# A fused encoder layer on one core: half of the attention's probability tiles turned by VectorE blocks and a trip through DRAM

## Chip, cores and metric

The kernel is one program on one core of a Trainium2 chip. The metric is the time of one execution on the device, in microseconds (us).

## What is computed

One hybrid encoder layer on 1024 tokens of width 1024, in float32. The change is in the second of its token mixers, attention over 8 heads:

```python
k_b = jnp.concatenate([k_nope, k_rope], axis=-1)
q_b = rmsnorm(q_b, q_head_norm)
k_b = rmsnorm(k_b, k_head_norm)
...
def attend(qblk):
    s = jnp.einsum('bhqd,bhkd->bhqk', qblk, k_t).astype(jnp.float32) * scale
    p = jax.nn.softmax(s, axis=-1)
    return jnp.einsum('bhqk,bhkd->bhqd', p.astype(v_t.dtype), v_t)
```

Around it stand, in this order: the latent projections, this attention, a gated linear attention (GLA) of 4 heads, the merge of both branches, and a mixture of 16 experts, which takes the largest share of the time.

## The kernel before

The kernel is written engine by engine: each engine has its own program, and engines wait for each other's counters (semaphores). Nothing is scheduled by a tool, so the order on each queue is the order of the code. SP's queue only issues DMAs, and a wait in it holds up every DMA behind it. P is 128, HALF 512, NT 8 tiles of 128 tokens, MH 8 heads.

Matmuls take each operand as a high and a low part (fp32r), three products for one: `three` (L1108 to L1110). So every operand has a `_hi` tile, rounded by ScalarE (ACT), and a `_lo` tile, the difference, made by VectorE (DVE) in `low_part` (L1719).

The attention loop goes over STEPS: (i, n) is head i, query tile n; tile t = 8i + n; five more steps (8, 0) to (8, 4) drain it. In one step:

- PE (TensorE) makes the scores of tile t, 10 matmuls of 128x512 into two PSUM banks (`scores`); transposes one piece of the coming head's q or k (`seam`); transposes the eight 128x128 blocks of tile t - 2 (`probs_T`, L1097); runs some key tiles of the product with the values of a finished half head (`values`, 3 matmuls a key tile); and projects a piece of a later head (`project`). In the drain, `project_qk` starts the GLA stage.
- DVE takes the row maximum of tile t (`row_maximum`, L1954), makes low parts, and in `normalise` (L1960, L1961) divides tile t - 1 by its row sums.
- ACT copies the transposed tile to pT_hi (`probs_high`, L2797) and makes the exponentials with the row sums (`exponentials`, L2805). A tile of probabilities is in one of three buffers.
- `head_out` copies a finished half head to obS, and SP stores it (`store_ob`, L794).

In the last head, SP loads the layer's input rows again, as one DMA of 4 MB (L810, `hT_again`, shown as carry), and the first GLA weights (d_raw, L742). At steps (7, 6) and (8, 0) ACT makes `dense_hi` and `rows_high` of them, DVE `dense_lo` and `rows_low`. After the last store of attention output, GpSimd (POOL) builds constants for GLA, for which PE waits.

The functions that the diff touches:

## Time and profile before

| | us |
|---|---|
| median of 3 runs | 1935.23 |
| lowest, highest | 1934.19, 1937.03 |
| the profiled execution's own time | 1936.58 |
| its span in the profile | 1934.7 |

The profile shows one execution. Its span is the time from the first to the last instruction; the time outside it is 1.9 us. The attention loop lies between some 123 and 538 us. Busy times of PE are modelled from a pipeline in which matmuls overlap, so the distance between starts tells the cost of one, not its length. The rows below are from a breakdown by stretch, from the list of waits, from groups of like instructions, and from the timeline.

### The profile page before, as it was taken

The page shows a single profiled execution, that of the slowest core. Times are in us where ns is not written, and L with a number is a line of the kernel's source. Part 1 is how long each engine was busy: PE and PEld are TensorE (multiplying, and loading weights), DVE is VectorE, ACT ScalarE, POOL GpSimd, SP SyncE. Part 2 cuts the span into 40 slices and gives each one's busy share as a digit, 9 for nine tenths or more (in the row PEclk, how much of TensorE's full clock was granted, in tenths as well). Part 3 has the DMA queues.
Part 4 walks back from the last instruction along what each step waited for, and adds up shares of the span by engine and source line. Part 5 has one row for each costly group of instructions (what it writes and reads, how often), then busy time and mean ns, then how long its engine had stood idle before and what let it go on. Part 6 is the DMA issues. An engine that isn't in the chain of part 4 may idle for free.

```text
span 1934.7 us, 27125 instructions
## 1 busy us (share of the span) xinstructions
PE 1885.0 (97%) x9427; PEld 1598.3 (83%) x9427; DVE 1388.8 (72%) x1941; ACT 1066.4 (55%) x1768; POOL 135.8 (7%) x147
## 2 busy tenths in 40 slices
PE   8999999999999999999999999995999999999998
PEld 8988888888878888888888888884788888888886
DVE  4578777777855656556866348746799898998986
ACT  6576565655552434344534123324677777877775
POOL 1021111011000000000000000000000101001010
PEclk9999999999999999999999999997999999999999
DMA  6110000000321202021353553534999999999993
GB/s 209 44 43 7 23 18 23 23 18 26 121 66 33 64 25 66 22 77 65 120 176 131 178 192 109 175 142 181 359 400 400 391 401 393 396 400 390 399 391 77
DMA packets 147482, 327.58 MB, mean 169 GB/s; under 512 B 18080, under 2 KB 72736, under 8 KB 147232
## 3 DMA queue, kind: packets, MB, share of 16 engines
q1 hardware_dynamic: 141600, 309.59, 43.0%
q0 software_dynamic: 4752, 16.78, 3.4%
q8 instruction: 57, 0.93, 0.2%
q14 instruction: 33, 0.27, 0.0%
q10 hardware_dynamic: 1040, 0.00, 0.0%
HBM read 287.92 MB, written 38.40 MB: 169 GB/s over the span
## 4 chain that ended last, share of the span: by engine, by line
PE 91%; DVE 5%; ACT 2%; issue 1%; DMA 1%; POOL 1%; SPq 0%; DVEq 0%; ACTq 0%; POOLq 0%
PE ps L1108 24%; PE ps L1110 24%; PE ps L1109 24%; PE ps L1097 7%; PE ps L1195 3%; PE ps L1403 1%; PE ps L1234 1%; PE ps L1233 1%; PE ps L1415 1%; PE ps L1387 1%; PE ps L1413 1%; DVE affT L2571 1%; DMA xs<-in_x 1%; DVE top_v L2564 0%; DVE pT_lo L1719 0%
## 5 line engine op out<-in xcount | busy, mean ns | idle before, releaser
L1719 DVE TENSOR_TENSOR w_lo<-w_raw,w_hi 128x1024 fp32r<-128x1024 f32 x384 | 442.7, 1219 | 54.8 <-ACT w_hi L3173 54.6
L3173 ACT ACTIVATE w_hi<-w_raw 128x1024 fp32r<-128x1024 f32 x384 | 371.1, 1053 | 0.4 <-PE ps L1110 0.4
L1108 PE MATMUL ps<-w_hi,xeT_hi 128*128 128x512 f32 x512 | 201.2, 393 | 1.0 <-DVE w_lo L1719 0.9
L1110 PE MATMUL ps<-w_hi,xeT_lo 128*128 128x512 f32 x512 | 199.7, 390 | 0.0
L1109 PE MATMUL ps<-w_lo,xeT_hi 128*128 128x512 f32 x512 | 199.2, 389 | 0.0
L1719 DVE TENSOR_TENSOR d_lo<-d_raw,d_hi 128x1024 fp32r<-128x1024 f32 (+1 forms) x66 | 67.1, 1027 | 124.5 <-ACT d_hi L2814 119.9
L1108 PE MATMUL ps<-hT_parts,d_hi 128*128 128x512 f32 x368 | 145.3, 395 | 0.0
L1110 PE MATMUL ps<-hT_parts,d_lo 128*128 128x512 f32 x368 | 143.9, 391 | 0.0
L1109 PE MATMUL ps<-hT_parts,d_hi 128*128 128x512 f32 x368 | 143.8, 391 | 0.0
L1015 POOL TENSOR_TENSOR stat<-stat,minus_half 128x4 f32<-128x4 f32 (+3 forms) x56 | 54.3, 971 | 1176.5 <-DVE stat L1716 1176.4
L1954 DVE TENSOR_REDUCE row_max<-ps 128x1 f32<-128x1024 f32 x64 | 78.3, 1224 | 79.1 <-PE ps L1234 79.0
L2814 ACT ACTIVATE d_hi<-d_raw 128x1024 fp32r<-128x1024 f32 x42 | 44.6, 1062 | 136.3 <-PE ps L1110 79.2
L1108 PEld LDWEIGHTS ps<-w_hi,xeT_hi 128*128 128x128 f32 x512 | 96.1, 188 | 21.3 <-DVE w_lo L1719 1.2
L1110 PEld LDWEIGHTS ps<-w_hi,xeT_lo 128*128 128x128 f32 x512 | 96.1, 188 | 20.4
L1108 PE MATMUL ps<-d_hi,hT_parts 128*128 128x512 f32 x288 | 112.6, 391 | 0.0
L1109 PEld LDWEIGHTS ps<-w_lo,xeT_hi 128*128 128x128 f32 x512 | 96.2, 188 | 19.5
L1109 PE MATMUL ps<-d_lo,hT_parts 128*128 128x512 f32 x288 | 112.1, 389 | 0.0
L1110 PE MATMUL ps<-d_hi,hT_parts 128*128 128x512 f32 x288 | 112.1, 389 | 0.0
L1108 PE MATMUL ps<-w_hi,act_T_hi 128*128 128x512 f32 x256 | 101.3, 396 | 0.8 <-ACT ye L3196 0.8
L1110 PE MATMUL ps<-w_hi,act_T_lo 128*128 128x512 f32 x256 | 99.9, 390 | 0.0
L1109 PE MATMUL ps<-w_lo,act_T_hi 128*128 128x512 f32 x256 | 99.6, 389 | 0.0
L1719 DVE TENSOR_TENSOR pT_lo<-ps,pT_hi 128x512 fp32r<-128x512 f32 x128 | 82.0, 682 | 0.7 <-ACT pT_hi L2797 0.2
(451 smaller groups left out, 4363.3 us busy)
## 6 DMA issues: line engine op xcount, KB each, us to landing
w_raw<-in_w_gate_e SPq DMA_DIRECT2D x128, 512.0 KB, 7.4
w_raw<-in_w_up_e SPq DMA_DIRECT2D x128, 512.0 KB, 7.1
w_raw<-in_w_down_e SPq DMA_DIRECT2D x128, 512.0 KB, 6.6
d_raw<-in_w_in SPq DMA_DIRECT2D x80, 256.0 KB, 3.3
gates_T<-stage SPq DMA_DIRECT2D x16, 512.0 KB, 2.7
sg<-gates_T SPq DMA_DIRECT2D x16, 512.0 KB, 3.7
stage<-mla_out_T SPq DMA_DIRECT2D x12, 512.0 KB, 5.2
xs<-in_x SPq DMA_DIRECT2D x8, 512.0 KB, 12.8
```

Source lines behind the costliest of these rows:

```text
L1015: pool.tensor_tensor(dst, dst, minus_half[:, 0:dst.shape[1]], ALU.pow).then_inc(done, 1)
L1097: ins = pe.transpose(ps[0:rows, bank, j * P:(j + 1) * P], src, ident[:])
L1108: pe.matmul(out_ap, a_hi, b_hi, start=start, stop=False)
L1109: pe.matmul(out_ap, a_hi, b_lo, start=False, stop=False)
L1110: return pe.matmul(out_ap, a_lo, b_hi, start=False, stop=stop)
L1195: mm = pe.matmul(out_ap, src[:, k, toks], w[:, k, :], start=k == 0, stop=k == kc - 1)
L1233: pe.matmul(bank, qr_T[:, q], kr_T[i % 2][:, cols], start=False, stop=False)
L1234: mm = pe.matmul(bank, qr_T[:, q], kr_lo[i % 2][:, cols], start=False, stop=True)
L1719: return dve.tensor_tensor(dst, whole, high.bitcast(F32), ALU.subtract)
L1954: dve.tensor_reduce(row_max[:, n:n + 1], ps[:, 2 * (n % 2):2 * (n % 2) + 2, :], mybir.AxisListType.XY, ALU.max, negate=True).then_inc(max_ ...
L2814: nc.scalar.activation(d_hi[:, n % 2, :], d_raw[:, n % 2, :], ACT.Copy).then_inc(d_hi_ok, 1)
L3173: nc.scalar.activation(w_hi[:, n % RING, :], w_raw[:, n % RAW, :], ACT.Copy).then_inc(hi_ok, 1)
```

## The change

Tiles with an even number up to 60 (31 of 64, `by_dma`) are no longer transposed by PE. DVE transposes their 32x32 blocks within each group of 32 partitions (`probs_squares`) into squares_T; SP stores squares_T to DRAM with four DMAs, one for each group of 32 partitions, and, when they have landed, loads the tile back from there in its turned order straight into pT_lo (`turn_probs`). Two steps later ACT rounds it to pT_hi (`turned_high`) and DVE makes pT_lo in place (`turned_low`). The other 33 tiles go on through PE, one step earlier than before (tile t - 1 at step t). pT_hi and pT_lo get a new layout, 16 groups of 32 queries outside, key tiles inside, so that `values` reads its 512 columns as 16 runs of 32.

`normalise` is gone. The inverses of the row sums are made for four tiles at once (`inverse_sums`), stored to DRAM, spread from there over all partitions (`store_inverse`, `spread_inverse`), and `head_out` multiplies with them. There are two buffers of probabilities in place of three. The rows for GLA are loaded as eight DMAs, each issued when the one before has landed (`load_rows`), and the first d_raw loads are issued at step (7, 6). Some counters of later stages reuse counters of the loop, which changes no order.

The core of the diff; left out are the declarations of semaphores, the reused counters, and waits that only take the new counts:

```diff
-def tile_at(i, n):
-    return 8 * i + n - 2 if 0 <= 8 * i + n - 2 < 8 * MH else None
+def by_dma(t):
+    return 0 <= t < 8 * MH - 2 and t % 2 == 0
+def by_tensor(t):
+    return 0 <= t < 8 * MH and not by_dma(t)
...
-                        probs = sb_in(head_mem, "probs", [P, 3, S])
-                        pT_hi = sb_in(head_mem, "pT_hi", [P, 2, NT, HALF], F32R)
-                        pT_lo = sb_in(head_mem, "pT_lo", [P, 2, NT, HALF], F32R)
+                        probs = sb_in(head_mem, "probs", [P, 2, S])
+                        squares_T = sb_in(head_mem, "squares_T", [P, Q4, NT, SQ])
+                        pT_hi = sb_in(head_mem, "pT_hi", [P, 2, Q4 * Q4, NT, SQ], F32R)
+                        pT_lo = sb_in(head_mem, "pT_lo", [P, 2, Q4 * Q4, NT, SQ], F32R)
...
+        def probs_part(tile, t):
+            q = t % NT
+            return tile[:, q // Q4, Q4 * (q % Q4):Q4 * (q % Q4) + Q4]
+        def inverse_at(h, half):
+            if (h, half) == (MH - 1, 1):
+                return squares_T[:, 0:2].rearrange("p j c a -> p (j c a)")
+            return obS[:]
...
+            def turn_probs(t):
+                d, group = t // 2, t // Q4
+                sp.wait_ge(sq_ok, d + 1)
+                rows = p_dram[d % SLOTS].rearrange("(j b) q x -> b j q x", b=SQ)
+                for q in range(Q4):
+                    sp.dma_start(rows[:, :, q, :],
+                                 squares_T[q * SQ:(q + 1) * SQ].rearrange("b j c a -> b j (c a)")).then_inc(p_out, 16)
+                sp.wait_ge(p_out, 16 * Q4 * (d + 1))
+                if d:
+                    sp.wait_ge(p_in, 16 * d)
+                if group >= 2:
+                    sp.wait_ge(pv_mm, group - 1)
+                sp.dma_start(probs_part(pT_lo, t).bitcast(F32),
+                             p_dram[d % SLOTS].rearrange("p q (c a) -> p q c a", a=SQ)).then_inc(p_in, 16)
+            def store_inverse(h, half):
+                m = 2 * h + half
+                sp.wait_ge(inv_ok, m + 1)
+                if m:
+                    sp.wait_ge(inv_in, 16 * m)
+                sp.dma_start(inv_dram[half].rearrange("(t p) -> p t", p=P), row_inv[:, Q4 * half:Q4 * half + Q4],
+                             allow_slow_non_contiguous=True).then_inc(inv_out, 16)
+            def spread_inverse(h, half):
+                m = 2 * h + half
+                sp.wait_ge(inv_out, 16 * m + 16)
+                if m and m < 2 * MH - 1:
+                    sp.wait_ge(ob_out, 16 * m)
+                sp.dma_start(inverse_at(h, half), spread(inv_dram[half], HALF)).then_inc(inv_in, 16)
+            def load_rows(k):
+                if k == 0:
+                    sp.wait_ge(h_out, 32)
+                    sp.wait_ge(seam_tr, MH * 8)
+                else:
+                    sp.wait_ge(hT_in, 16 * k)
+                sp.dma_start(hT_again[:, k, :], h_dram[k]).then_inc(hT_in, 16)
+            load_ukv(2)
+            for i, n in STEPS:
+                if i < MH and by_dma(8 * i + n - 1):
+                    turn_probs(8 * i + n - 1)
+                if (i, n) == (MH - 2, 0):
                     sp.wait_ge(prj_mm, group_count(MH - 1, 7))
                     sp.wait_ge(gate_io.sem, gate_io.at(16))
                     sp.dma_start(gateT[0:STACK].bitcast(F32), gate_dram).then_inc(gate_io.sem, 16)
-                if i:
+                if n == 0 and i:
+                    store_inverse(i - 1, 1)
+                    if i == MH:
+                        spread_inverse(i - 1, 1)
+                if n == 2 and i:
                     store_ob(i - 1, 0)
-                if i + 2 < MH:
-                    load_uq(i + 2)
-                if i == MH - 1:
-                    sp.wait_ge(h_out, 32)
-                    sp.wait_ge(seam_tr, MH * 8)
-                    sp.dma_start(hT_again, h_dram.rearrange("k p s -> p k s")).then_inc(hT_in, 16)
-                if i:
-                    store_ob(i - 1, 1)
-            load_gla(0, 0)
-            load_gla(0, 1)
-            store_ob(MH - 1, 0)
+                    if i < MH:
+                        spread_inverse(i - 1, 1)
+                if n == 4:
+                    if i + 2 < MH:
+                        load_uq(i + 2)
+                    if i + 3 < MH:
+                        load_ukv(i + 3)
+                    if i < MH:
+                        store_inverse(i, 0)
+                    if 0 < i < MH:
+                        store_ob(i - 1, 1)
+                if n == 6:
+                    spread_inverse(i, 0)
+                if n == 6 and i == MH - 1:
+                    load_gla(0, 0)
+                    load_gla(0, 1)
+                if n % 2 == 0 and 8 * (MH - 1) + 2 <= 8 * i + n:
+                    for k in range(2):
+                        if 8 * i + n - 8 * (MH - 1) - 2 + k < KD:
+                            load_rows(8 * i + n - 8 * (MH - 1) - 2 + k)
             store_ob(MH - 1, 1)
...
             def probs_T(t):
-                pe.wait_ge(p_ok, t + 1)
+                pe.wait_ge(exp_ok, t + 1)
+                before = [u for u in range(t) if by_tensor(u)]
                 for b in range(2):
-                    if t:
-                        pe.wait_ge(pt_lo, 2 * t + b - 1)
+                    if before:
+                        pe.wait_ge(pt_lo, parts_count(before[-1]) - 1 + b)
                     else:
                         pe.wait_ge(seam_lo, seam_count(0, 1) + b)
-                    transpose4(4 + b, P, [probs[:, t % 3, (4 * b + j) * P:(4 * b + j + 1) * P]
+                    transpose4(4 + b, P, [probs[:, t % 2, (4 * b + j) * P:(4 * b + j + 1) * P]
                                           for j in range(4)]).then_inc(p_tr, 1)
...
-                               pT_hi[:, half, k, :], pT_lo[:, half, k, :], k == 0, k == NT - 1)
+                               pT_hi[:, half, :, k, :], pT_lo[:, half, :, k, :], k == 0, k == NT - 1)
...
-                if tile_at(i, n) is not None:
-                    probs_T(tile_at(i, n))
+                if by_tensor(8 * i + n - 1):
+                    probs_T(8 * i + n - 1)
...
-            def normalise(t):
-                n = t % NT
+            def inverse_sums(h, half):
+                m = 2 * h + half
+                dve.wait_ge(exp_ok, NT * h + Q4 * half + Q4)
+                if m >= 2:
+                    dve.wait_ge(inv_out, 16 * (m - 1))
+                at = slice(Q4 * half, Q4 * half + Q4)
+                dve.reciprocal(row_inv[:, at], row_sum[:, at]).then_inc(inv_ok, 1)
+            def probs_squares(t):
                 dve.wait_ge(exp_ok, t + 1)
-                s.link(dve.reciprocal(row_inv[:, n:n + 1], row_sum[:, n:n + 1]))
-                dve.tensor_scalar(probs[:, t % 3, :], probs[:, t % 3, :], row_inv[:, n:n + 1], None,
-                                  ALU.mult).then_inc(p_ok, 1)
+                if t:
+                    dve.wait_ge(p_out, 16 * Q4 * (t // 2))
+                dve.transpose(squares_T[:], probs[:, t % 2, :].rearrange("p (c j b) -> p j c b", c=NT, j=Q4)) \
+                    .then_inc(sq_ok, 1)
             def probs_low(t):
                 q = t % NT
                 for b in range(2):
-                    dve.wait_ge(pt_hi, 2 * t + b + 1)
-                    at = (slice(None), q // 4, slice(4 * b, 4 * b + 4), slice((q % 4) * P, (q % 4 + 1) * P))
-                    low_part(pT_lo[at], ps[:, 4 + b, :].rearrange("p (a c) -> p a c", a=4),
-                             pT_hi[at]).then_inc(pt_lo, 1)
+                    dve.wait_ge(pt_hi, parts_count(t) - 1 + b)
+                    part = probs_part(pT_lo, t)[:, :, 4 * b:4 * b + 4].rearrange("p q k a -> p k q a")
+                    high = probs_part(pT_hi, t)[:, :, 4 * b:4 * b + 4].rearrange("p q k a -> p k q a")
+                    low_part(part, ps[:, 4 + b, :].rearrange("p (k q a) -> p k q a", k=4, q=Q4), high).then_inc(pt_lo, 1)
+            def turned_low(t):
+                dve.wait_ge(pt_hi, parts_count(t))
+                low = probs_part(pT_lo, t)
+                low_part(low, low.bitcast(F32), probs_part(pT_hi, t)).then_inc(pt_lo, 1)
             def head_out(h, j):
                 dve.wait_ge(pv_mm, 2 * h + j + 1)
                 if h or j:
                     dve.wait_ge(ob_out, 32 * h + 16 * j)
-                dve.tensor_copy(obS[:], ps[:, 6, :]).then_inc(ob_ev, 1)
+                dve.wait_ge(inv_in, 32 * h + 16 * j + 16)
+                dve.tensor_tensor(obS[:], ps[:, 6, :], inverse_at(h, j), ALU.mult).then_inc(ob_ev, 1)
...
-            END_STEP = (MH - 1, 7)
             for i, n in STEPS:
-                if (i, n) == END_STEP:
-                    probs_low(tile_at(i, n))
+                t = 8 * i + n
+                if by_dma(t - 1):
+                    probs_squares(t - 1)
                 if i < MH:
                     row_maximum(i, n)
                     if seam_at(i, n):
                         seam_low(*seam_at(i, n))
-                if tile_at(i, n) is not None and (i, n) != END_STEP:
-                    probs_low(tile_at(i, n))
-                if tile_at(i, n + 1) is not None and (i, n) not in (END_STEP, (MH, 0)):
-                    normalise(tile_at(i, n + 1))
-                if (i, n) in ((MH - 1, 6), END_STEP):
-                    normalise(tile_at(i, n + 2))
+                if by_tensor(t - 1):
+                    probs_low(t - 1)
+                if by_dma(t - 3):
+                    turned_low(t - 3)
+                if n == 0 and i:
+                    inverse_sums(i - 1, 1)
+                if n == 4 and i < MH:
+                    inverse_sums(i, 0)
...
             def probs_high(t):
-                q = t % NT
                 for b in range(2):
-                    act.wait_ge(p_tr, 2 * t + b + 1)
-                    at = (slice(None), q // 4, slice(4 * b, 4 * b + 4), slice((q % 4) * P, (q % 4 + 1) * P))
-                    nc.scalar.activation(pT_hi[at], ps[:, 4 + b, :].rearrange("p (a c) -> p a c", a=4),
+                    act.wait_ge(p_tr, 2 * tensor_count(t) - 1 + b)
+                    part = probs_part(pT_hi, t)[:, :, 4 * b:4 * b + 4].rearrange("p q k a -> p k q a")
+                    nc.scalar.activation(part, ps[:, 4 + b, :].rearrange("p (k q a) -> p k q a", k=4, q=Q4),
                                          ACT.Copy).then_inc(pt_hi, 1)
+            def turned_high(t):
+                act.wait_ge(p_in, 16 * (t // 2) + 16)
+                nc.scalar.activation(probs_part(pT_hi, t), probs_part(pT_lo, t).bitcast(F32), ACT.Copy).then_inc(pt_hi, 1)
             def exponentials(i, n):
                 t = 8 * i + n
                 act.wait_ge(max_ok, t + 1)
-                if t >= 3:
-                    act.wait_ge(p_tr, 2 * (t - 3) + 2)
-                nc.scalar.activation(probs[:, t % 3, :].rearrange("p (a c) -> p a c", a=2),
+                if by_dma(t - 2):
+                    act.wait_ge(sq_ok, (t - 2) // 2 + 1)
+                elif t >= 2:
+                    act.wait_ge(p_tr, 2 * tensor_count(t - 2))
+                if i and n % Q4 == 0:
+                    act.wait_ge(inv_ok, 2 * i - 1 + n // Q4)
+                nc.scalar.activation(probs[:, t % 2, :].rearrange("p (a c) -> p a c", a=2),
...
-                if tile_at(i, n) is not None:
-                    probs_high(tile_at(i, n))
+                t = 8 * i + n
+                if by_tensor(t - 1):
+                    probs_high(t - 1)
+                if by_dma(t - 3):
+                    turned_high(t - 3)
```

Three places in the queues, at the end of the loop. First DVE, in head 7. pT_lo, d_lo and hT_parts are low parts. Before, from the row maximum of tile 62:

```order
L1954 TENSOR_REDUCE row_max<-ps 128x1 [waits s_mm]
L1719 TENSOR_TENSOR pT_lo<-ps,pT_hi 128x4x128 [waits pt_hi] x2
L1960 RECIPROCAL row_inv<-row_sum 128x1 [waits exp_ok]
L1961 TENSOR_SCALAR probs<-probs,row_inv 128x1024 [waits head_step]
L1960 RECIPROCAL row_inv<-row_sum 128x1 [waits exp_ok]
L1961 TENSOR_SCALAR probs<-probs,row_inv 128x1024 [waits head_step]
L1719 TENSOR_TENSOR d_lo<-d_raw,d_hi 128x1024 [waits d_hi_ok]
L1988 SCALAR_TENSOR_TENSOR hT_parts<-carry,g_mix_c,hT_parts 128x1024 [waits hT_hi_ok]
L1719 TENSOR_TENSOR pT_lo<-ps,pT_hi 128x4x128 [waits pt_hi] x2
L1954 TENSOR_REDUCE row_max<-ps 128x1 [waits s_mm]
L1960 RECIPROCAL row_inv<-row_sum 128x1 [waits exp_ok]
```

With the change, from the block transpose of tile 60:

```order
L2057 STREAM_TRANSPOSE squares_T<-probs 128x1024 [waits p_out,exp_ok]
L2042 TENSOR_REDUCE row_max<-ps 128x1 [waits s_mm]
L1807 TENSOR_TENSOR pT_lo<-pT_lo,pT_hi 128x1024 [waits pt_hi]
L2042 TENSOR_REDUCE row_max<-ps 128x1 [waits s_mm]
L1807 TENSOR_TENSOR pT_lo<-ps,pT_hi 128x4x4x32 [waits pt_hi] x2
L1807 TENSOR_TENSOR d_lo<-d_raw,d_hi 128x1024 [waits d_hi_ok]
L2090 SCALAR_TENSOR_TENSOR hT_parts<-carry,g_mix_c,hT_parts 128x1024 [waits hT_hi_ok]
L2042 TENSOR_REDUCE row_max<-ps 128x1 [waits s_mm]
L1807 TENSOR_TENSOR pT_lo<-ps,pT_hi 128x4x4x32 [waits pt_hi] x2
L1807 TENSOR_TENSOR pT_lo<-pT_lo,pT_hi 128x1024 [waits pt_hi]
L1807 TENSOR_TENSOR pT_lo<-ps,pT_hi 128x4x4x32 [waits pt_hi] x2
L2051 RECIPROCAL row_inv<-row_sum 128x4 [waits inv_out,exp_ok]
```

The scalings of probs are gone, the row maximum of tile 63 stands behind d_lo and hT_parts as before, and the low parts of tile 61 have moved ahead of d_lo, those of tile 62 behind that row maximum.

Second, SP's queue. carry is the rows' buffer (hT_again), obS the attention output. Before, from the stores of heads 5 and 6 on:

```order
L794 DMA mla_out_T<-obS 128x512 x3
L810 DMA carry<-rows_T 128x8x1024
L794 DMA mla_out_T<-obS 128x512
L742 DMA d_raw<-in_w_in 128x4x128 x4
L794 DMA mla_out_T<-obS 128x512 x2
L742 DMA d_raw<-in_w_in 128x2x256 x8
L770 DMA w_a<-in_gla_wa_f 16x128 x3
```

With the change, from the store of head 6's second half on:

```order
L829 DMA mla_out_T<-obS 128x512
L867 DMA carry<-rows_T 128x1024 x2
L836 DMA probs_T<-squares_T 32x4x256 x4
L843 DMA pT_lo<-probs_T 128x1024
L859 DMA obS<-inverse_sums 128x512
L777 DMA d_raw<-in_w_in 128x4x128 x4
L867 DMA carry<-rows_T 128x1024 x2
L851 DMA inverse_sums<-row_inv 128x4x1
L859 DMA squares_T<-inverse_sums 128x512
L867 DMA carry<-rows_T 128x1024 x2
L829 DMA mla_out_T<-obS 128x512 x2
L777 DMA d_raw<-in_w_in 128x2x256 x8
```

The first d_raw loads, which stood right behind the store of head 6's second half, now stand behind two loads of rows, the whole turn of tile 60 and a spread of inverse sums, and the last two stores of obS stand behind the last rows.

Third PE, the last transposes of probs. Before, from the middle of the first project_qk:

```order
L1108 MATMUL ps<-hT_parts,d_hi 128x512 [waits exp_ok]
L1109 MATMUL ps<-hT_parts,d_hi 128x512
L1110 MATMUL ps<-hT_parts,d_lo 128x512
L1108 MATMUL ps<-hT_parts,d_hi 128x512
L1109 MATMUL ps<-hT_parts,d_hi 128x512
L1110 MATMUL ps<-hT_parts,d_lo 128x512
L1097 MATMUL ps<-ident,probs 128x128 [waits pt_lo,p_ok]
L1097 MATMUL ps<-ident,probs 128x128 x3
L1097 MATMUL ps<-ident,probs 128x128 [waits pt_lo]
L1097 MATMUL ps<-ident,probs 128x128 x3
L1108 MATMUL ps<-pT_hi,v_hi 128x512
```

With the change, from the last key tile of step (7, 7):

```order
L1195 MATMUL ps<-pT_hi,v_hi 128x512
L1196 MATMUL ps<-pT_lo,v_hi 128x512
L1197 MATMUL ps<-pT_hi,v_lo 128x512
L1184 MATMUL ps<-ident,probs 128x128 [waits pt_lo,exp_ok]
L1184 MATMUL ps<-ident,probs 128x128 x3
L1184 MATMUL ps<-ident,probs 128x128 [waits pt_lo]
L1184 MATMUL ps<-ident,probs 128x128 x3
L1195 MATMUL ps<-pT_hi,v_hi 128x512
```

The transposes of tile 63 stood behind project_qk; they now stand ahead of it and directly behind the values of step (7, 7), and wait for the exponential in place of the scaled tile.

## Rows read from the trace of the kernel before

**Rows 1.** The page: busy time of each engine, and the chain that ended last, by engine.
```profile
PE 1885.0 (97%) x9427; PEld 1598.3 (83%) x9427; DVE 1388.8 (72%) x1941; ACT 1066.4 (55%) x1768; POOL 135.8 (7%) x147
...
PE 91%; DVE 5%; ACT 2%; issue 1%; DMA 1%; POOL 1%; SPq 0%; DVEq 0%; ACTq 0%; POOLq 0%
```

**Rows 2.** Busy time by stretch (us, instructions), then granted clock, DMA share, GB/s.
```profile
165.00:480.00 315.00, 314.53 (x1865) 278.90 (x1864) 242.05 (x441) 186.86 (x479) 33.30 (x24) 1.00 0.07 21
480.00:495.00 15.00, 15.00 (x86) 12.77 (x85) 14.11 (x27) 8.10 (x15) 0.00 (x0) 1.00 0.00 1
511.00:546.00 35.00, 32.47 (x160) 26.24 (x159) 26.62 (x34) 20.41 (x28) 3.62 (x6) 0.99 0.28 83
```

**Rows 3.** The waits, 127 to 527 us: in total, times, longest.
```profile
DVE row_max L1954 <- PE ps L1234: 79.0, 54, 3.6
...
PE ps L1097 <- DVE probs L1961: 0.7, 2, 0.5
```

**Rows 4.** Groups by line and form, 127 to 527 us: busy us, mean ns, idle before.
```profile
L1719 DVE TENSOR_TENSOR pT_lo<-ps,pT_hi 128x512 fp32r<-128x512 f32 x126 | 80.7, 682 | 0.7 <-ACT pT_hi L2797 0.2
L1954 DVE TENSOR_REDUCE row_max<-ps 128x1 f32<-128x1024 f32 x64 | 78.3, 1224 | 79.1 <-PE ps L1234 79.0
...
L2797 ACT ACTIVATE pT_hi<-ps 128x512 fp32r<-128x512 f32 x126 | 68.1, 597 | 13.1 <-PE ps L1097 13.0
L1097 PE MATMUL ps<-ident,probs 128*128 128x128 f32 x504 | 65.7, 273 | 1.1 <-DVE probs L1961 0.7 <-DVE pT_lo L1719 0.4
...
L1961 DVE TENSOR_SCALAR probs<-probs,row_inv 128x1024 f32<-128x1024 f32 x64 | 49.1, 767 | 2.3
...
L1960 DVE RECIPROCAL row_inv<-row_sum 128x1 f32<-128x1 f32 x64 | 9.8, 154 | 1.3 <-ACT probs L2805 1.3
...
L1910 DVE TENSOR_TENSOR qR<-qR,q_cos 128x128 f32<-128x128 f32 x14 | 4.0, 288 | 0.2
```

**Rows 5.** The chain that ended last, end of the loop: start, us, what.
```profile
506.57 0.88 PE ps L1097 x8
...
537.76 0.70 DVE obS L1976
```

**Rows 6.** Timeline of PE in step 58: start us, us, engine, line, operation.
```profile
495.91 1.03 PE L1097 MATMUL ps<-ident,probs 128*128 128x128 f32 x8
496.70 0.48 PE L1108 MATMUL ps<-pT_hi,v_hi_even 128*128 128x512 f32 x1
497.02 0.39 PE L1109 MATMUL ps<-pT_lo,v_hi_even 128*128 128x512 f32 x1
```

**Rows 7.** Timeline of DVE, end of the loop.
```profile
518.71 1.22 DVE L1719 TENSOR_TENSOR d_lo<-d_raw,d_hi 128x1024 fp32r<-128x1024 f32 x1
```

**Rows 8.** Timeline of ACT, end of the loop.
```profile
517.22 1.07 ACT L2814 ACTIVATE d_hi<-d_raw 128x1024 fp32r<-128x1024 f32 x1
```

**Rows 9.** Timeline of SP's queue, end of the loop.
```profile
495.86 0.32 SPq L794 DMA_DIRECT2D mla_out_T<-obS  x1
...
510.88 2.13 SPq L742 DMA_DIRECT2D d_raw<-in_w_in  x4
```

**Rows 10.** DMA issues of the whole span: count, KB each, median us to landing.
```profile
d_raw<-in_w_in SPq DMA_DIRECT2D x80, 256.0 KB, 3.3
...
mla_out_T<-obS SPq DMA_DIRECT2D x16, 256.0 KB, 2.2
...
carry<-rows_T SPq DMA_DIRECT2D x4, 512.0 KB, 5.3
...
pos_i<-in_positions SPq DMA_DIRECT2D x1, 4.0 KB, 4.3
```

**Rows 11.** Busy time by stretch, around two waits of PE.
```profile
543.00:545.10 2.10, 0.17 (x2) 0.04 (x1) 1.26 (x2) 1.06 (x1) 1.41 (x2) 1.00 0.30 104
545.10:548.98 3.88, 3.88 (x10) 3.05 (x11) 2.42 (x2) 1.54 (x2) 0.00 (x0) 0.56 0.00 0
...
134.90:137.00 2.10, 0.45 (x2) 0.01 (x1) 1.93 (x2) 2.05 (x11) 0.00 (x0) 1.00 0.64 221
```

72 lines of the change are left out of this document (42 added, 30 removed).

## Prediction

> **What bounds the kernel now.** I read the page's busy shares first: TensorE (PE) is busy 97% of the span and is 91% of the chain that ended last [rows 1]. The attention loop is the stretch that the change edits, so I then read the busy time by stretch [rows 2]: from 165 to 480 us PE is busy 314.5 of 315 us, VectorE (DVE) 242, ScalarE (ACT) 187, and the DMA share is 0.07. So whatever leaves PE's queue there is gained, as long as nothing else grows into the wait. The waits say the same from the other side: row_max waited 79.0 us for PE's scores in 54 of 64 tiles, while PE waited 0.7 us for the normalised tiles [rows 3]. The reader should look at two places where the cover is thin: 480 to 495 us, where PE's steps are short and DVE is busy 14.1 of 15 us, and the end of the loop, 511 to 546 us, where PE is idle 2.5 us in all [rows 2].
>
> **What is removed from PE.** The transposes of a tile are eight matmuls. Their mean of 273 ns overlaps the next ones [rows 4]; the price is the piece in the chain, 0.88 us for eight [rows 5], and the same comes from start times: transposes start at 495.91, the next matmul at 496.70 and the one after at 497.02, where the usual distance is 0.23, so 0.79 + 0.32 - 0.23 = 0.88 [rows 6]. I take 0.87. Tiles 0, 2, ..., 60 go by DMA: 31 tiles, 31 x 0.87 = 27.0 us.
>
> **What changes on DVE and ACT.** For a pair of tiles DVE loses two scalings (0.77 each) and two reciprocals (0.15) [rows 4], 1.8 us. It swaps one pair of 0.68 pT_lo pieces for one 1024-wide subtraction: 1.22 by the d_lo row of the same form [rows 7], so -0.1. It gains one 32x32-block transpose of 128x1024, which no row shows. Its bounds are 0.77 (one source, 1024 wide) and 2.5 (twice the 1.22 of a 1024-wide reduction, if four-byte elements went at half rate); I take 1.25, since reduction and subtraction, 1024 elements each, both cost 1.22. Sum: -0.7 us a pair. ACT swaps two 0.60 copies for one of about 1.06 (the d_hi row [rows 8]): nothing. So with 0.87 off PE and 0.7 off DVE, both shrink together over most of the loop and the 79 us of slack stay. The permuted writes of pT_hi and pT_lo have runs of 32 elements. The q_cos rows have such runs (4 of 32) and cost 0.29 us for 128 elements; contiguous 1024 cost 1.22, which makes 1.04 ns an element and 0.16 fixed, and the 512-wide pT_lo rows of 0.68 lie on the same line [rows 4, 7]. Short runs add nothing that shows: nothing.
>
> The Trainium skill ("VectorE: DVE Perf Modes", The three transpose paths) gives 311 ns for a 128x128 bf16 block transpose on VectorE and 390 ns on TensorE, and advises TensorE for a full 128x128. By eight of its figures the new instruction would be an estimated 2.5 us and DVE would gain 0.6 us a pair in place of losing 0.7; by its figure for TensorE the removed work would look like 3.1 us, which this trace refutes with 0.88 for the pipelined eight [rows 5].
>
> **The round trip through DRAM.** Per tile SP issues four stores and a load. One issue is about 0.35 us (0.32 for the store of mla_out_T [rows 9], which has as many pieces), and that 256 KB store lands in 2.2 us [rows 10]. Trip: 4 x 0.35 + 2.2 + 0.35 + a 512 KB load; 256 KB loads of d_raw land in 3.3 us [rows 10], I take 3.5: 7.5 us. The tile is turned at the head of step t+1 and wanted on ACT in step t+3. A step is now some 5.7 us (315 us for about 51 tiles is 6.2, less half of 0.87). From the end of the scores of t: exponential done at about 3.7, block transpose at 5.2, and the copy on ACT is due at 3 x 5.7 + 0.6 = 17.7. That leaves 12.5 us for 7.5. In the short steps after 480 us (10 us a pair now, 9.1 after) it is still 3 x 4.6 + 0.6 - 5.2 = 9.2. The single buffer squares_T and the in-order SP queue hold too: what stands ahead of each turn waits only for work of the step before. Hidden, at nothing. The sums' store has 512 four-byte pieces; the nearest row is pos_i, 1024 of them, 4.3 us to landing [rows 10]. It has three steps of cover; at the end it is issued at about 528 and its spread has landed by 537, three before the last output copy wants it. Nothing.
>
> **480 to 495 us.** A pair of steps is 10 us on PE and 9.4 on DVE. After: 9.1 and 8.7, with DVE's queue in order and its transpose ahead of row_max. Average cover is 0.4 us a pair. I charge 1.0 us here and for the DVE-bound first five steps together (0 if the cover holds, 3 if the transpose costs 2.5).
>
> **The end of the loop.** Here I follow the new order, on the clock of the kernel before. At 493.6 (495.91 less ten matmuls of 0.23 [rows 6]) step 58 begins; 28 turned tiles lie behind, a lead of 28 x 0.87 = 24.4 us. With 2.3 us for scores, 0.7 for each key tile of values and 0.87 for transposes: the scores of 60 end at 505.6, of 61 at 510.1, of 62 at 512.4. DVE: row_max(60) to 506.8, exponential to 508.8, block transpose(60) to 510.0, row_max(61) to 511.3, exponential to 512.6. PE waits 0.2, transposes 61, does two key tiles (514.9), scores 63 (517.2), transposes 62 and two key tiles: 519.5. Then its next work is the transposes of 63; before, it had values and project_qk in between.
> What is late is exp(63). The first d_raw load, which was issued at 510.88 [rows 9], now stands on SP behind tile 60's turn: stores from 510.0 to 511.4, landed 513.6, load and spread issued 514.3, two d_raw issues of 0.53 (2.13/4 [rows 9]) 515.4, landed with 3.5 us at 518.9. ACT makes d_hi (520.0) and hT_hi (521.1), DVE d_lo (521.2) and hT_lo (522.4), and only then comes row_max(63), to 523.6, and exp(63), to 524.9. PE is idle 5.4 us. From there: transposes 0.87, two key tiles 1.4, project_qk 2.8, two key tiles 1.4, project_qk 2.8, eight key tiles 5.6: 539.8, where before they ended at 537.6 (the output copy starts at 537.76 [rows 5]). The end costs 2.2 of the lead of 24.4. The tail behind it (output copy, store, POOL's constants) moves as a whole.
> An idle PE also costs clock: with 0.17 us of work in 543.0 to 545.1 the granted clock in the next 3.88 us was 0.56, the lower level of 1.2 GHz, and eight matmuls took about 0.43 in place of 0.23 each, 1.6 us; with 0.45 of work in 134.9 to 137.0 it stayed at 1.00 [rows 11]. 5.4 us is the longer gap by far, so I charge 1.6.
>
> **Sum.** 24.4 - 2.2 - 1.0 - 1.6 = 19.6 us. The profiled execution took 1936.6 for a span of 1934.7, so it would read 1917.0 with a span of 1915.1. The median of the runs shown is 1935.2, 1.4 below it; the forecast on that scale is 1915.6, say 1916. Stages behind shift unchanged: what they load is released by their own progress.
>
> **Rivals.**
> - *The gap at the end is shorter* (0.12). If d_raw lands early, exp(63) still stands behind the two copies and two subtractions: about 2 us idle and no fall of the clock. For it speaks that landings of 3 us are usual; against it SP's order. Gain 19.6 + 3.4 + 1.6 = 24.6: 1910 or 1911.
> - *DVE becomes the bound in short steps* (0.08). A block transpose of 2.5 us costs 0.6 us a pair over today; over most of the loop PE's 11.5 us a pair still covers DVE's 10, but in the last head's steps and the first ones, and in the gap at the end, 3 to 5 us are lost more: 1920.
> - *The round trip is late* (0.07). If stores and loads landed in 5.3 us, as 512 KB loads of rows_T did later in the program [rows 10], the trip is 1.75 + 10.6 = 12.4 us: level with the normal steps' 12.5 and 3.2 us late in some five short ones, 16 us: 1932. Every further microsecond costs some 25 us. Against it: the DMA share of 0.07.
> - *PE reads the turned layout more slowly* (0.09), the one on the other side. The values matmuls now read 16 runs of 32 columns that lie 1 KB apart. 384 matmuls are touched, 0.233 us apart now; at 0.051 us more each the gain is gone, at twice the time they add 384 x 0.233 = 89 us and the kernel takes 2005. No matmul of this trace reads such an operand, so nothing bounds it but that.
> The Trainium skill ("Advanced Engine Details and Errata", SBUF Cachelines) puts a penalty on accesses that find a new 16-byte line each time and says two hits on a line absorb it; runs of 32 four-byte elements have four hits a line, so by it the 89 us are 0. Its sentence that any non-contiguous pattern slows matmuls stands under PSUM.
> - *Freed time is not on the path*: excluded by 0.5 us of PE idle in 315 [rows 2].
>
> **How the numbers follow.** The forecast, gain 15 to 23 us, has 0.64. Its own range is 1912 to 1921. From 1908 (all 27.0 us, no gap) to 1928 (gap and late trips together) the range holds it, the first two rivals and half of the third: 0.85. A measurement tells about 0.2%, 4 us. Faster by more than that: 0.64 + 0.12 + 0.08 + half of 0.07 = 0.87; within it 0.04; slower 0.09, the operand's pattern and very late trips.
>
> **What would show it.** 264 in place of 512 transposes of probs, still 0.87 us for eight. STREAM_TRANSPOSE 31 times at about 1.25 us. Values matmuls still 390 ns long and 0.23 us apart. No waits of ACT for pT_lo's load in mid-loop. row_max(63) late behind d_lo, PE idle some 5 us before the last transposes of probs, and a granted clock under 1 after that. Wrong would be: values matmuls over 0.25 us apart, repeated waits of ACT for the turned tiles, or DVE without idle time ahead of row_max.

## The result, and the profile after

The changed kernel takes 1961.49 us (median of 4 runs, 1960.49 to 1961.68), beside 1934.72 us of the kernel before in the same session: ratio 1.0135, 95% interval 1.0117 to 1.0153. It is 27 us slower where 19 us less was forecast. The profiled execution took 1961.58 us for a span of 1959.3 us.

The page of the changed kernel: busy time of PE, the DMA share in 40 slices of 49 us, and the chain by engine.

```profile
PE 1869.9 (95%) x9179; PEld 1574.2 (80%) x9179; DVE 1373.2 (70%) x1829; ACT 1066.3 (54%) x1737; POOL 135.3 (7%) x147
...
DMA  6125454554621111111454544343999999999993
...
PE 84%; DVE 6%; DMA 5%; ACT 2%; issue 1%; SPq 1%; POOL 1%; DVEq 0%; ACTq 0%; POOLq 0%
```

PE lost 15 us of busy time, but its share of the chain fell from 91% to 84% and DMA's rose from 1% to 5% [rows 1]. Where, the windows say (columns as in [rows 2]):

```profile
165.00:480.00 315.00, 308.99 (x1723) 264.58 (x1723) 240.52 (x373) 191.83 (x465) 33.30 (x24) 1.00 0.50 113
480.00:495.00 15.00, 14.20 (x68) 11.27 (x66) 9.44 (x10) 4.92 (x8) 0.00 (x0) 1.00 0.49 86
511.00:546.00 35.00, 15.85 (x66) 13.26 (x67) 13.51 (x15) 14.41 (x20) 0.00 (x0) 0.71 0.55 128
```

In mid-loop PE now idles 6 us of 315, and the DMA share is 0.50 where it was 0.07 [rows 2]. From 511 to 546 us PE idles 19 us and its clock falls to 0.71. Groups of the loop, 127 to 527 us, by form (busy us, mean ns, then idle time before it and what ended it):

```profile
L2057 DVE STREAM_TRANSPOSE squares_T<-probs 128x1024 f32<-128x1024 f32 x31 | 38.4, 1240 | 12.7 <-DMA probs_T<-squares_T 12.3 <-issue 0.3
L1807 DVE TENSOR_TENSOR pT_lo<-pT_lo,pT_hi 128x1024 fp32r<-128x1024 f32 x30 | 36.7, 1224 | 12.3 <-ACT pT_hi L2905 11.3
L1184 PE MATMUL ps<-ident,probs 128*128 128x128 f32 x256 | 35.0, 282 | 9.8 <-ACT probs L2916 9.8
L2905 ACT ACTIVATE pT_hi<-pT_lo 128x1024 fp32r<-128x1024 f32 x30 | 31.6, 1053 | 23.9 <-DMA pT_lo<-probs_T 23.9
L1196 PE MATMUL ps<-pT_lo,v_hi_even 128*128 128x512 f32 x64 | 25.9, 404 | 0.0
```

The new instructions cost what was forecast: 1.24, 1.22 and 1.05 us. What is new stands behind the second bar: ACT waited 23.9 us for turned tiles, and DVE 12.3 us for squares_T to be stored. The chain from 503 us on (start, us, what):

```profile
503.46 3.45 DMA probs_T<-squares_T
...
508.34 11.62 DMA carry<-rows_T
...
521.76 3.65 DMA probs_T<-squares_T
...
526.77 5.86 DMA d_raw<-in_w_in
...
532.65 1.06 ACT d_hi L2925
...
542.02 8.02 DMA inverse_sums<-row_inv
550.06 0.32 SPq L859
550.38 0.04 issue
550.42 6.39 DMA carry<-rows_T
556.84 0.32 SPq L867
557.15 0.05 issue
557.20 4.11 DMA mla_out_T<-obS
```

All large pieces are transfers: a row load of 11.6 us behind a store of inverses (issued at 507.36), d_raw, and then 8.0 us until a store of 2 KB has landed (is written, as its semaphore tells), a row load behind it, and the last attention output behind that.

The start of each tile's exponential (rows of ACT's timeline) is a clock for the loop. Against the kernel before, in us, with three of the experiments below:

| tile | after | sums only | 16 pieces | 16 pieces and order |
|---|---|---|---|---|
| 16 | -3.3 | +1.5 | -2.2 | -3.2 |
| 32 | -6.9 | +2.9 | -6.6 | -7.6 |
| 52 | -12.4 | +3.5 | -12.2 | -13.2 |
| 59 | -5.7 | +3.2 | -13.5 | -14.5 |
| 61 | -1.1 | +3.4 | -11.1 | -15.2 |
| 63 | +13.8 | +14.8 | -2.9 | -14.1 |

Up to tile 52 the changed kernel leads by 12.4 us. From there to the last exponential it loses 26 us, and 9 more until GLA's first constants are ready (w_a_split, at 544.53 us before and 567.62 after). About 2 of these 9 are no delay: in the new order more of PE's work stands behind the last exponential, and the fast version without tile 60 (below) also leads by 16.3 us there and by 14.1 at w_a_split.

### The profile page after: what moved, and what is told of

The parts are those of the page before. It is cut to its first block, busy times and chain, and to the rows that moved or that the text cites. A ratio compares the mean times of both kernels' runs of the same rounds, so it can differ in the third digit from the quotient of the medians.

```text
span 1959.3 us, 26754 instructions
## 1 busy us (share of the span) xinstructions
PE 1869.9 (95%) x9179; PEld 1574.2 (80%) x9179; DVE 1373.2 (70%) x1829; ACT 1066.3 (54%) x1737; POOL 135.3 (7%) x147
## 4 chain that ended last, share of the span: by engine, by line
PE 84%; DVE 6%; DMA 5%; ACT 2%; issue 1%; SPq 1%; POOL 1%; DVEq 0%; ACTq 0%; POOLq 0%
PE ps L1195 23%; PE ps L1197 23%; PE ps L1196 23%; PE ps L1184 5%; PE ps L1282 3%; PE ps L1491 1%; DMA probs_T<-squares_T 1%; PE ps L1503 1%; DMA carry<-rows_T 1%; PE ps L1321 1%; PE ps L1320 1%; DVE row_max L2042 1%; PE ps L1475 1%; PE ps L1501 1%; SPq L836 1%
## 5 line engine op out<-in xcount | busy, mean ns | idle before, releaser
L1195 PEld LDWEIGHTS ps<-hT_parts,d_hi 128*128 128x128 f32 x368 | 69.8, 190 | 14.8 <-issue 0.4
```

Source lines behind the costliest of these rows:

```text
L1195: pe.matmul(out_ap, a_hi, b_hi, start=start, stop=False)
```

## The experiments

Theories: **A**, the store of the row sums' inverses is slow and everything behind it on the DMA queues is late. **B**, the turn's own traffic is too much for the short steps. **C**, the order on SP's queue in the last head: each row load waits for the landing of the one before, in front of turns, weights and the last stores. In the sessions of these runs the kernel before had medians of 1935.1 to 1936.5 us; every ratio is to its own session.

### What the store of the sums costs

**128 pieces of 16 bytes** in place of 512 of four:

```diff
-sp.dma_start(inv_dram[half].rearrange("(t p) -> p t", p=P), row_inv[...]
+sp.dma_start(inv_dram[half].rearrange("(p t) -> p t", p=P), row_inv[...]
```

> The inverse sums are stored in the order in which they lie (four neighbours of a partition together): the same 2 KB in 128 pieces of 16 bytes in place of 512 of 4. The outputs' rows are scaled by the wrong sums. Theory A (the store of 512 four-byte pieces keeps the DMA queue for some 8 us, and what stands behind it on the queue is late by that): it lands in about 3 us in place of 8, the four stores behind it in 3.6 us in place of 8, ACT's 23.9 us of waiting for turned tiles and its 16 us wait for d_raw shrink to under 10 together, and the kernel takes 1925 to 1935. Rival B (the turn's own 1 MB a tile is too slow for the short steps of the last heads): no change, 1957 to 1962. Rival C (SP's order at the end: weights behind rows and turns): at most 5 us, 1955 to 1961.

1937.72 us, ratio 1.0012 (1.0002 to 1.0022). One rearrangement of 2 KB (the rows are scaled by the wrong sums; the bytes are the same) takes back 24 of the 27 us, with all turns in place. That is 3 us above A's range and far below the others': A holds for most of the loss, and B, the turn's own traffic, doesn't make it.

**16 pieces of 128 bytes**, which keeps the output whole:

```diff
+dve.transpose(inv_T[:], row_inv[:])
...
+for j in range(Q4):
+    sp.dma_start(inv_dram[half].rearrange("(t j b) -> j t b", j=Q4, b=SQ)[j], inv_T[SQ * j:SQ * j + Q4, :])
```

> The inverses of the sums of four tiles are transposed by DVE (128x32, in 32x32 blocks) and stored as 16 pieces of 128 bytes by four DMAs, in place of 512 pieces of four bytes; the output is complete. Theory A (the store of 512 four-byte pieces keeps the DMA queues busy about 8 us each time, and all that is queued behind it is late): like the kernel with 128 pieces, 1934 to 1941 us, because 24 of the 26 us of loss went with the pieces there. Theory C (the rest is lost by the order on SP's queue in the last head, where each load of rows waits for the landing of the one before): the same time here, since the order is untouched, with ACT still waiting 6 to 10 us for turned tiles 58 and 60. Theory B (the turn's own traffic is too much for the short steps): 1950 or more.

1938.24 us, 1.001 (1.0 to 1.0019), in A's range. The rows of SP's queue show the follower. In the changed kernel the turn behind a store of inverses (start, us; L836 the four stores of the turn, L843 its load, which waits for their landing):

```profile
171.17 0.38 SPq L851 DMA_DIRECT2D inverse_sums<-row_inv  x1
172.58 2.38 SPq L836 DMA_DIRECT2D probs_T<-squares_T  x4
182.44 0.34 SPq L843 DMA_DIRECT2D pT_lo<-probs_T  x1
```

and with 16 pieces:

```profile
172.60 1.61 SPq L853 DMA_DIRECT2D inverse_sums<-inv_T  x4
174.26 2.03 SPq L837 DMA_DIRECT2D probs_T<-squares_T  x4
178.15 0.34 SPq L844 DMA_DIRECT2D pT_lo<-probs_T  x1
```

9.9 us from the first store to the load, against 3.9. It is so at each of the 14 turns behind or around such a store: 7.6 to 10.3 us, against 3.7 to 4.4 with 16 pieces.

**Each store twice**, the second to a place that nobody reads:

```diff
+for copy in (inv_dram, inv_dram_2):
+    sp.dma_start(copy[half].rearrange("(t p) -> p t", p=P), row_inv[...]
```

> Each store of the row sums' inverses (512 four-byte pieces) is issued twice, the second into another place in DRAM that nobody reads. Theory A (the pieces occupy the DMA queues for about 8 us, and what is queued behind is late by that): 16 more such stretches, those in the loop partly under cover, those in the last head not: 1975 to 2010 us. If what counts is only the time until the sums themselves have landed, and other transfers pass beside them: 1960 to 1968 us.

1971.96 us, 1.019 (1.0174 to 1.0205): 10 us more, between the two expectations. The DMA share from 120 to 450 us rose from 0.49 to 0.63 at no more bytes, and ACT's waits for turned tiles (120 to 575 us) to 33.4 us. The direction is A's, the size was overrated. That much of the second store falls into cover is a guess; the spread of the sums also waits for both copies here.

**On ACT's queue:**

```diff
+if (n == 1 and 0 < i < MH) or (i, n) == (MH, 0):
+    store_inverse(i - 1, 1)    # nc.scalar.dma_start
+if n == 5 and i < MH:
+    store_inverse(i, 0)
```

> The changed kernel, its 512 four-byte pieces issued on ACT's queue in place of SP's, one step later in the loop. If the pieces hold up what stands behind them on the same queue only: 1935 to 1945 us, like the kernels with 128 and 16 pieces. If they occupy the DMA engines for every queue: 1955 to 1970 us, like the changed kernel.

2004.84 us, 1.0354 (1.0338 to 1.037), far above both. ACT issues the pieces at 154.00:

```profile
154.00 0.37 ACTq L2900 DMA_DIRECT2D inverse_sums<-row_inv  x1
```

and on SP's queue the stores of the turn that had begun just before are not all landed for 13 us (12.5 to 13.4 in eight such turns):

```profile
152.88 1.80 SPq L836 DMA_DIRECT2D probs_T<-squares_T  x4
166.15 0.34 SPq L843 DMA_DIRECT2D pT_lo<-probs_T  x1
```

Another queue is no way out: the pieces hold up SP's transfers too. (The Trainium skill, "DMA: Bandwidth & Descriptors", Issuing engines are not separate DMA queues, says that all issuers share the same 16 engines; the 13 us agree.) Why it costs more than on SP's queue no run separates. The waits fit this: the pieces now meet the stores of a turn already under way, so the turned tile comes later, and DVE must wait for those stores before its next block transpose (120 to 600 us):

```profile
ACT pT_hi L2893 <- DMA pT_lo<-probs_T: 53.3, 9, 8.9
DVE squares_T L2045 <- DMA probs_T<-squares_T: 40.8, 8, 6.8
...
PE ps L1183 <- DVE qr_T L1795: 31.4, 7, 7.5
```

**128 pieces of four bytes:** from the second head on only one tile of each four is stored.

```diff
+n = Q4 if m < 2 else 1
-..., row_inv[:, Q4 * half:Q4 * half + Q4]
+..., row_inv[:, Q4 * half:Q4 * half + n]
```

> The changed kernel, but from the second head on each store of inverses takes one tile's 128 pieces of four bytes in place of four tiles' 512; the output lacks the other three tiles' sums (old ones stand in for them). If the number of pieces sets the time of the store (some 8 us for 512): 2 us for 128, covered, so 1935 to 1943 us, like 128 pieces of 16 bytes. If the four bytes of a piece are what is slow, each store keeps most of its time and the kernel stays at 1950 to 1962 us.

**The same, 512 bytes apart in DRAM:**

```diff
+sp.dma_start(inv_apart[half][:, 0:1], row_inv[:, Q4 * half:Q4 * half + 1]
```

> As the kernel with 128 pieces of four bytes a store, but the pieces go to places 512 bytes apart in DRAM that nobody reads; the output stands on old sums from the second head on. If pieces of four bytes are slow by themselves: landing in some 8 us again and 1955 to 1962 us. If they are slow because neighbours fall side by side: landing in 2 to 3 us and 1935 to 1943 us.

**128 pieces of eight bytes:** `n = Q4 if m < 2 else 2`, rearranged as "(p t) -> p t".

> Each store from the second head on takes two tiles' inverses as 128 pieces of eight bytes; the output lacks the other two tiles' sums and has their order wrong. If only four-byte pieces are slow: landing in 2 to 3 us and 1935 to 1943 us. If the price ends at 16 bytes: landing in some 8 us and 1955 to 1962 us. If it falls with the size: between, 1943 to 1955 us.

The three took 1960.4 (ratio 1.0126, 1.0109 to 1.0142), 1938.82 (1.0014, 1.0004 to 1.0023) and 1942.69 us (1.0037, 1.0023 to 1.0051). DMA issues from 197 to 450 us (count, KB each, median us to landing), first of the kernel with four-byte pieces side by side:

```profile
inverse_sums<-row_inv SPq DMA_DIRECT2D x10, 0.5 KB, 8.2
```

of the one with four-byte pieces 512 bytes apart:

```profile
inverse_sums_apart<-row_inv SPq DMA_DIRECT2D x10, 0.5 KB, 1.4
```

of the one with eight-byte pieces:

```profile
inverse_sums<-row_inv SPq DMA_DIRECT2D x10, 1.0 KB, 2.9
```

and of the first experiment, 16-byte pieces:

```profile
inverse_sums<-row_inv SPq DMA_DIRECT2D x10, 2.0 KB, 1.4
```

The first stays in the range for slow four-byte pieces, but the second shows that it is not the four bytes: 1.4 us when apart. Nor is it the count: 128 pieces cost the kernel as much as 512, which land in 8.0 us in the chain above and in 8.9 to 9.0 at the same place of three other runs. The third lands, by time and landing, in the range of "only four-byte pieces are slow", though it is still twice as long as the 16-byte one and 4 us slower in the kernel. What is slow is writing small pieces that lie side by side in DRAM: from start to start four bytes 8.2 us, eight 2.9, sixteen 1.4. In these three the size of a piece and the distance grow together; only for four bytes were they separated. The Trainium skill ("DMA: Bandwidth & Descriptors", Specifications) says that transfers under 512 bytes are done as read-modify-write; by that alone all four would cost alike, and they cost 1.4 to 8.2 us. How the distance comes into it was not measured.

### What the order on SP's queue costs

**The first d_raw loads two steps earlier**, (7, 4) in place of (7, 6), slow pieces kept:

> The first two d_raw loads are issued at step (7, 4), behind the store of head 6's second half, as in the kernel before, and not behind the turn of tile 60. A: they stand right behind a sums' store and land some 10 us after their issue, still 10 to 14 us earlier than now: 1946 to 1952. B: the same gain or less, 1946 to 1958. C: all of the loss in the last head goes: 1930 to 1938.

1962.05 us, 1.0137 (1.012 to 1.0154): nothing, outside all three ranges. The turn of tile 60 now stood behind a row load that took 15.4 us to land, behind a store of inverses and the weights.

**The whole new order**, slow pieces kept: those loads at (7, 4), and the rows in pairs, which now also stand at other steps, behind the turns of tiles 58 and 60 and no longer ahead of them:

```diff
-    sp.wait_ge(hT_in, 16 * k)
-sp.dma_start(hT_again[:, k, :], h_dram[k])
+    sp.wait_ge(hT_in, 32 * k)
+for r in (2 * k, 2 * k + 1):
+    sp.dma_start(hT_again[:, r, :], h_dram[r])
...
+if (i, n) in ((MH - 1, 3), (MH - 1, 6), (MH, 0), (MH, 2)):
+    load_rows(...)
```

> The order of the last head alone, with the 512 four-byte pieces kept. Theory C (the order carries 10 to 15 us of the loss by itself): 1946 to 1952 us. Theory A with C as a follower (the order costs only what stands in front of the pieces, and with the slow store still in the queue something else is late): 1955 to 1962.

1956.65 us, 1.0103 (1.0088 to 1.0119): 5 us, in the range of A with C as a follower.

**16 pieces and the order:**

> The 16 pieces, and the order on SP's queue in the last head: the rows are loaded as four pairs that wait only for the pair before, spread from step (7, 3) to (8, 2), and the first d_raw loads are issued at (7, 4). Theories A and C together: the waits of ACT for turned tiles 58 and 60 and for d_raw go, about 8 + 8 us less their overlap, so 1920 to 1930 us. Theory A alone (order is worth nothing): 1934 to 1941, as without the order. Theory B: 1945 or more.

1927.12 us, 0.9957 (0.9943 to 0.997), faster than the kernel before, as A and C together say. On 16 pieces the order is worth 11 us, on 512 only 5: with slow stores left, something else is late.

**Its two parts alone**, on 16 pieces: rows in pairs, and weights early.

> The kernel with 16 pieces (1938 us), and of the new order in the last head only the rows' loads in four pairs. If the single row loads, each waiting for the landing of the one before, hold up the turns of tiles 58 and 60 behind them: most of the 11 us, so 1928 to 1932 us. If the d_raw loads at (7, 6) are what ACT waits for: 1935 to 1939 us.

> The kernel with 16 pieces (1938 us), and of the new order only the d_raw loads at (7, 4) in place of (7, 6). If the rows' loads carry the loss: 1935 to 1939 us. If the d_raw loads carry it: 1928 to 1932 us.

1932.16 (0.9979, 0.997 to 0.9989) and 1934.58 us (0.9994, 0.9984 to 1.0004), from 1938.24: 6 and 4 us, which add up to about the 11. Both lie within 0.5 us of the ranges in which the rows' loads carry most of it: the rows are the larger part, d_raw's place the smaller. Whether the pairing or the later place of the rows counts was not separated. SP's queue shows C as such, with 16 pieces and the old order:

```profile
487.36 4.96 SPq L869 DMA_DIRECT2D carry<-rows_T  x2
492.37 1.93 SPq L837 DMA_DIRECT2D probs_T<-squares_T  x4
```

The second row load of L869 waits for the first one's landing, and tile 58's stores wait behind it until 492.37. With the new order they go at 486.30, ahead of the rows:

```profile
486.30 1.89 SPq L837 DMA_DIRECT2D probs_T<-squares_T  x4
491.36 0.34 SPq L844 DMA_DIRECT2D pT_lo<-probs_T  x1
491.80 0.85 SPq L870 DMA_DIRECT2D carry<-rows_T  x2
```

### What the turn costs and brings

**Turn only:** `normalise` restored, no sums through DRAM.

> The turn of 31 tiles stays; the sums' way through DRAM is gone and every tile is scaled in place by VectorE ahead of its transpose, as in the kernel before. VectorE gets 1.8 us a pair of tiles back to do. A: 1925 to 1940. B: 1957 or more, since the turn is as it was. C: 1950 to 1960.

1950.48 us, 1.008 (1.0063 to 1.0097), just inside C's range. Of PE's 17.8 us of waiting for probabilities 14.0 fall behind 480 us, where SP's order is the old one and ACT waited 6.5 us for d_raw: C. From 165 to 480 us DVE, which keeps its 1.8 us a pair and gets the block transpose on top, is busy 277 of 315 us, and PE idles 7.6; row_max waited only 32.4 us for PE in place of 79.0 [rows 3]. The kernel with 16 pieces has the same order and the same turns without the scalings, and takes 12 us less: the turn needs the scalings gone.

**Sums only:** `by_dma` false for all tiles.

> No tile is turned by DMA: all 64 go through TensorE; the sums' way through DRAM, the two buffers and SP's order at the end stay. A: the loop up to the last head as before (within 3 us), but rows and d_raw behind the sums' stores are late at the end: 1940 to 1950. B: as the kernel before, 1933 to 1938. C: 1940 to 1950 too.

1964.53 us, 1.0151 (1.0134 to 1.0168), no theory's range either: without a single turned tile the kernel loses as much. In the last steps a row load behind a store of inverses took 12.9 us, and ACT waited 13.4 us for d_raw.

**The same with 16 pieces and the order:**

> Pieces and order as in the kernel with both (1927 us), but no tile is turned through DRAM: all go through PE, and only the normalisation is left out and the sums divided at the output. If the turn is worth what its transposes cost on PE less its side costs (0.56 us a turned tile in the loop, 31 of them, 17 us): 1940 to 1945 us. If the removal of the normalisation, not the turn, brings the gain: 1925 to 1932 us.

1938.57 us, 1.0015 (1.0005 to 1.0024), a little under the 1940 to 1945. Store and order together are 26 us of the sums-only kernel. Against 1927.12 the turn is worth 11 us (15 against the version without tile 60, below), and leaving out the normalisation alone gains nothing.

**Block transpose later:**

```diff
-if by_dma(t - 1):
-    probs_squares(t - 1)
 if i < MH:
     row_maximum(i, n)
     if seam_at(i, n):
         seam_low(*seam_at(i, n))
+if by_dma(t - 1):
+    probs_squares(t - 1)
```

> The 16 pieces and the order, and DVE makes the block transpose (1.24 us) behind the row maximum and the low part of the seam in place of ahead of them. If the short waits of PE's projections for DVE (about 0.85 us a head, the seam's low part is late) come from the block transpose in front: 3 to 6 us less than the kernel with pieces and order, and those waits gone. If the round trip has too little cover, the later start shows as waits of ACT for the turned tile, and the time is the same or longer.

1929.98 us, 0.9961 (0.9948 to 0.9975), not less than 1927.12. PE's waits for DVE from 140 to 470 us stayed (4.0 us, then 4.6), and ACT waited 11.7 us for turned tiles (120 to 575 us) in place of 5.0. So the second branch holds, as far as 3 us within overlapping intervals tell. The first reading, that the transpose's place in DVE's queue makes PE's waits, falls; what makes them stays open.

**Tile 60 through PE, and tiles 58 and 60:** `8 * MH - 4` and `8 * MH - 6` in `by_dma`. With 16 pieces and the order PE still stood before the last transposes:

```profile
510.62 1.97 PE L1185 MATMUL ps<-ident,probs 128*128 128x128 f32 x8 [4.95 <-ACT probs L2919]
```

> The kernel with 16 pieces and the new order, and tile 60 goes through PE (30 tiles turned in place of 31). There ACT waited 2.97 us for the turned tile 60 and PE 4.95 us for the last exponential, after which its clock stood at half for 2.6 us. If the round trip has too little cover in the short steps of the last head (the prediction's rival of a late round trip): the wait of PE goes or falls under 2 us, which gives 3 to 5 us and costs 0.6 us for the transposes back on PE, so 1922 to 1925 us. If PE would wait there for something else anyway (the row maximum, the rows' parts on ACT): 1926 to 1929.

> As the one without tile 60, and tile 58 goes through PE as well (29 turned). Late round trip in the short steps: as without 60, or 1 us more or less, since tile 58 had its cover already. If the traffic at the end as a whole delays the last steps: some 2 us less than without 60.

1923.17 (0.9941, 0.9927 to 0.9955) and 1922.88 us (0.9934, 0.9921 to 0.9948). Without tile 60:

```profile
508.44 1.09 PE L1185 MATMUL ps<-ident,probs 128*128 128x128 f32 x8 [1.61 <-ACT probs L2919]
```

The wait is 1.6 us, and the eight transposes take 1.09 us instead of 1.97, at the full clock. Tile 60's trip had too little cover, tile 58's had enough. In the kernel with pieces and order the trip took, from its first store to the landing of its load, 6.9 to 7.7 us up to tile 56, 8.8 at tile 58 and 9.8 at tile 60, where the prediction saw 9.2 us of cover. These two are the fastest versions here, 12 us under the kernel before.

## Why the prediction was wrong

**The step that failed: the sums' store, "Nothing".** It priced 512 four-byte pieces by pos_i, 4.3 us to landing [rows 10]. That row is a load, which reads such pieces from DRAM; this is a store that writes them side by side, and it takes 8.0 to 9.0 us. And I asked only whether the sums have cover for their own landing (in the loop they have), not what stands behind them: the turns took 7.6 to 10.3 us to their load in place of 3.7 to 4.4. That is the error of kind: 24 of the 46 us between forecast and result, by the runs with 128 and 16 pieces.

**SP's order at the end.** I followed the one thing that stands behind tile 60's turn, d_raw, and left out what stands in front of turns: the row loads, each waiting for a landing. On 16 pieces the rows are worth 6 us, d_raw's place 4, both 11; on slow pieces the longest of these waits grew to the 11.6 us in the chain. Had I listed SP's queue row by row, as I did for DVE, it would have been seen.

**27.0 us for the transposes: a size.** Four heads without any wait before, and with 16 pieces and the order, from tile 16's exponential to tile 48's (columns as in [rows 2]):

```profile
224.68:439.38 214.70, 214.70 (x1282) 190.85 (x1281) 164.07 (x297) 128.33 (x334) 22.20 (x16) 1.00 0.08 23
```

```profile
221.48:427.28 205.80, 204.22 (x1154) 175.64 (x1153) 158.63 (x249) 127.70 (x317) 22.20 (x16) 1.00 0.41 115
```

8.9 us for 16 turned tiles, 0.56 each in place of 0.87. From starts of matmuls in the same stretches, the transposes are 12.7 us, 0.79 each: the 0.09 that I added for the longer distance behind the next matmul did not go with them. The rest: other matmuls cost PE 2.2 us more, and PE waits 1.6 us. Over 31 tiles 0.56 each is 17 us in place of 27.0.

**PE reads the turned layout:** the rival's size is about 0.004 us a matmul (the spacing went from 0.233 to 0.237), where 0.051 decided. It is one part of those 2.2 us; that the layout causes it was not isolated. The Trainium skill's rule ("Advanced Engine Details and Errata", SBUF Cachelines), by which such runs are not slow, agrees with it.

**DVE and ACT:** right, 1.24 us for the block transpose (taken 1.25). The Trainium skill's figure ("VectorE: DVE Perf Modes", The three transpose paths), which made it 2.5 us, doesn't carry over to this form: the measurement decides. That DVE and PE shrink together holds only with the normalisation gone.

**The round trip, 7.5 us:** right in mid-loop, where with 16 pieces and the order the load is issued mostly 3.7 us after the first store and lands in 3.3, 6.9 to 7.7 us in all; too short in the last head, 8.8 and 9.8. "What stands ahead of each turn waits only for work of the step before" is false in the last head, and behind a store of the sums everywhere. The late-trip rival named the place, the short steps, and put 1932 us on it; its cause, a trip that is slow by itself, shows in part at tile 60 (9.8 us), which costs 4 us. The rest of the lateness came from what stands ahead on the queue.

**The end of the loop:** the forecast had exp(63) behind d_raw, PE idle 5.4 us and a fall of the clock for 1.6 us. In the changed kernel the wait was 17.4 us, as d_raw was issued at 526.29, not from 514.3 on. With 16 pieces and the old order it was still 10.7 us, ACT waiting 9.5 for d_raw: the mechanism is as forecast, at twice the size. With the order mended too it was 4.95 us, and the clock was at 0.50, its lower level, from 510 to 515 us. That this is near 5.4 is luck: there ACT waited 2.97 us for tile 60 and 0.9 for d_raw.

The sum by the runs, each step with some 2 us of noise between sessions: forecast 1916; 7 more for the transposes' size and the side costs, which is the 1923 without tile 60; 4 for tile 60; 11 for the order; 23 for the pieces: 1961.

## What to carry to other kernels

Before a small store goes onto a shared queue, ask in what pieces it lands in DRAM, how far apart, and price it by a store of the same pattern; then ask what stands behind it, not only who waits for it. A transfer that waits for another's landing is a wait of the whole queue: where a change puts new round trips on it, list that queue in order for the last, shortest steps. Cover counts where it is thinnest: the last tile of the loop is better left on the old path.

## What the runs showed of the hardware

- A store to DRAM of 128 four-byte pieces, one from each partition, lands in 8.2 us when neighbours lie four bytes apart in DRAM, in 1.4 us when they lie 512 bytes apart; eight-byte pieces side by side take 2.9 us, 16-byte ones 1.4. 512 four-byte pieces side by side take about the same as 128, 8.0 to 9.0 us at the end of the loop (10.4 and 10.8 in the first head of one run). By which mechanism was not measured.
- During such a store other transfers are late too. From the first of four 128 KB stores to the load that waits for them it took 7.6 to 10.3 us with the small pieces ahead on the same queue, 12.5 to 13.4 us with the pieces issued from ACT's queue just behind them, and 3.7 to 4.4 us with 16 pieces of 128 bytes.
- A 128x1024 float32 STREAM_TRANSPOSE costs DVE 1.24 us, as a subtraction of that size does (1.22), and TensorE reads 16 runs of 32 columns at almost full pace (a matmul of 512 columns each 0.237 us in place of 0.233).
